# Expert rows added up in pairs on four quarter-size tiles of TensorE's array, in a two-layer hybrid backbone

## The chip, the cores and the metric

The kernel runs on one core of one Trainium2 chip. The metric is the device time of one execution in microseconds (us); of several runs the median is given.

## What is computed

The reference is two layers of a backbone for 128 context tokens and 512 latent tokens of width 1024 (640 tokens, five tiles of 128). Each layer has attention, latent attention and a DeltaNet ahead of one output projection, and then an expert retrieval, which is the part that matters here. All data are float32. Cut to that part:

```python
def peer_ffn(h, w_pq, peer_keys, peer_u, peer_v):
    ...
    experts = jnp.take_along_axis(cand_ix, pos, axis=-1)
    gates = jax.nn.softmax(best, axis=-1)
    def block(args):
        tb, eb, gb = args
        act = jax.nn.gelu(jnp.einsum('nd,nhkd->nhk', tb, peer_u[eb]))
        return jnp.einsum('nhk,nhkd->nd', gb * act, peer_v[eb])
    ...
x = x + gt2 * peer_ffn(h, p['w_pq'], p['peer_keys'], p['peer_u'], p['peer_v'])
```

Every token takes 8 heads x 16 = 128 experts out of 16384. Each expert has a row of 1024 numbers of `peer_u` and a row of 1024 numbers of `peer_v`. The dot product of token and `peer_u` row, through a gelu and times the gate, is the weight with which the `peer_v` row is added to the token's sum.

## The kernel before

A layer is a series of blocks: modulation and projections, DeltaNet, attention, and last `tail`, which holds the output projection, the routing (queries, scores, the choice of experts) and the loop over the experts. `build` calls `tail` for each of the two layers; `finish` follows after the second and computes the final norm.

**The loop over rows.** A "row" of the kernel is one expert for each of the 128 tokens of a token tile: 128 partitions x 2048 numbers (the `peer_u` part in columns 0 to 1023, the `peer_v` part in columns 1024 to 2047), 1 MB. There are ROWS = 640 rows in a layer. They are held in SLOT = 9 buffers, `p.slots[n % 9]` (the trace names them `left` and `right`). A unit is UNIT = 32 rows that are added into the same sum of 128 x 1024; there are UNITS = 20 units in a layer. For row n the engines do this:

- POOL (L1379) waits until row n-9 is released (semaphore `row_free`) and issues the gather of row n as an indirect DMA.
- DVE (L1464) waits for the landing, and computes the 128 dot products into one column of `dot` (128 x 1024 elements read). Behind it comes the product of gelu and gate for the row before, `weigh(n - 1)` (L1440), and then one of the 16 pieces of the choice of experts for a later row group (`top_piece`, L1254 to L1298).
- ACT (L1548) applies the gelu, and then for the row before writes the diagonal (L1541): the identity times the 128 weights, one of DIAGS = 8 buffers of 128 x 128.
- PE (L1646) multiplies the diagonal with the two 512-column halves of the `peer_v` part and adds them into two PSUM banks. The trace shows two MATMUL and two LDWEIGHTS records for each of these matmuls, so four of each for a row. The last one raises `row_free`.

The order on PE is written out by hand: `routing_steps` gives a list of steps and the row ahead of which each is done. A query step (L1602, 8 matmuls of 128 x 512 for the latent tokens) stands ahead of rows 4, 20, 36 and 52 of each block of 128 rows, from the second block on, and at 44, 56, 68 and 80 in the first block. Score steps (L1614) stand ahead of rows 68, 84, 100 and 116, small query steps of 128 columns for the context tokens ahead of some of the first 40 rows. ACT copies a step's result out in `evacuate`, four rows later in its own loop. SP loads the query weights `wq` (L1360, 512 KB each), one buffer of four being free after each step.

**The end of a unit.** Unit u adds into PSUM banks 0 and 1 if u is even and into banks 2 and 3 if u is odd (`sum_banks`). In its loop DVE comes at row 8 of the next unit to `add_unit`: two products of a bank with the gate row `gt2` (L1455, 128 x 512 each) into `y`, and the addition of `y` to the residual `x` (L1457, 128 x 1024). PE waits ahead of the first row of unit u (u of 2 or more) for `y_read` of unit u-2.

Lines that the prediction's steps touch besides: L1509 and L1515 (ACT's copies of 128 x 512 out of PSUM), L1060 and L1062 (score matmuls of the attention; for the differential heads, `kTa` and `qTa`, they use 32 partitions of the contraction, a different group of 32 for each of two following maps), L1089 (a matmul with a 64-column stationary operand), and L234, ACT's 128 x 1024 square at the start of the next layer.

Of the kernel before, what the change touches and what calls it, by code (L numbers as in the profile page):

```python
# [29 lines left out]
ALU = mybir.AluOpType  # L30
# [3 lines left out]
P = 128  # L34
D, L = 1024, 2
# [26 lines left out]
C = 4  # L62
# [1244 lines left out]
def tail(p, lay):  # L1307
# [20 lines left out]

        return c if g == 0 else C + (NT - 1) * c + t - 1

    def sum_banks(u):

        return ps[2 * (u % 2)], ps[2 * (u % 2) + 1]

    def query_bank(m):

# [6 lines left out]
    with nc.Block() as block:  # L1343
        @block.sync
        def _(sp):
            for g in range(2):
                spread(sp, p.rows[:, 0, g, :], d["mid_rows"][0][g:g + 1, :], "load_gt1")
            for g in range(2):
                spread(sp, p.rows[:, 1, g, :], d["mid_rows"][2][g:g + 1, :], "load_sc2")
            spread(sp, p.g2row, d["g_norm2"][bass.ds(lay, 1)], "load_sc2")  # L1350
            for g in range(2):
                spread(sp, p.rows[:, 2, g, :], d["mid_rows"][1][g:g + 1, :], "load_sh2")
            sp.dma_start(p.keysT[:, :], d["keysT"][bass.ds(lay, 1)].rearrange("l p n -> p (l n)")).then_inc(sem("load_keys"), 16)
            for i in range(8 * C):
                if i >= WR:
                    sp.wait_ge(sem("pq_mm"), i - WR + 1)
                if i == 6 * C:
                    sp.wait_ge(sem("y_read"), 2 * C)
                    spread(sp, p.gt2, d["mid_rows"][3][1:2, :], "load_gt2s")
                sp.dma_start(p.wq[:, i % WR, :, :], d["w_pq"][bass.ds(lay, 1), i % (4 * C)].rearrange("l p k n -> p (l k) n")  # L1360
                             ).then_inc(sem(f"load_q{i % WR}"), 16)
                if i == 7:
                    spread(sp, p.gt2, d["mid_rows"][3][0:1, :], "load_gt2")
            for name in p.front_sems:
                sp.sem_clear(sem(name))
# [18 lines left out]
        def _(dve):  # L1384
# [58 lines left out]
            def add_unit(u):  # L1443

                t, _ = unit_of(u)
                dve.wait_ge(sem("row_free"), UNIT * (u + 1))
                if u == 0:
                    dve.wait_ge(sem("load_gt2"), 16)
                if u == C:
                    dve.wait_ge(sem("load_gt2s"), 16)  # L1450
                for c, bank in enumerate(sum_banks(u)):
                    cols = slice(c * 512, c * 512 + 512)
                    if u >= 1:
                        dve.wait_ge(sem("residual"), u)
                    nc.vector.tensor_tensor(p.y[:, cols], bank, p.gt2[:, cols], ALU.mult).then_inc(sem("y_read"), 1)  # L1455
                dve.wait_ge(sem("y_read"), 2 * u + 2)
                nc.vector.tensor_tensor(p.x[:, t, :], p.x[:, t, :], p.y[:, :], ALU.add).then_inc(sem("residual"), 1)  # L1457

            for n in range(ROWS):
# [17 lines left out]
        @block.scalar  # L1477
        def _(act):
            for t in range(NT):
                act.wait_ge(sem("m_turned"), t + 1)  # L1480
                nc.scalar.activation(p.mixedT[t],
                                     ps[t % 2].rearrange("p (k n) -> p k n", k=4), ACT.Copy).then_inc(sem("m_out"), 1)

            def square(t):
                act.wait_ge(sem("res1"), 2 * t + 2)
                nc.scalar.activation(p.junk[:, :], p.x[:, t, :], ACT.Square, accum_out=p.ss1[:, t:t + 1]).then_inc(sem("square2"), 1)
                act.wait_ge(sem("square2"), t + 1)
                nc.scalar.activation(p.rt1[:, t:t + 1], p.ss1[:, t:t + 1], ACT.Sqrt, bias=p.eps[:, 0:1], scale=1.0 / D).then_inc(sem("root2"), 1)

            def turned(t):  # L1490
                act.wait_ge(sem("h2_turned"), t + 1)
                for h in range(2):
                    nc.scalar.activation(p.h2T[:, 4 * h:4 * h + 4, t * P:(t + 1) * P],  # L1493
                                         ps[h].rearrange("p (k n) -> p k n", k=4), ACT.Copy).then_inc(sem("h2T_out"), 1)

            def evacuate(j):

                kind, g, c, i = steps[j]
                if kind == "q":
                    m = block_of(g, c, i)  # L1500
                    act.wait_ge(sem("pq_mm"), m + 1)
                    if g == 0:
                        if c >= 2:
                            act.wait_ge(sem("sc_mm"), c - 1)
                        nc.scalar.activation(p.qp0[:, c % 2, i, :], query_bank(m)[:, 0:P], ACT.Copy).then_inc(sem("q_out"), 1)
                    else:
                        if c >= 1:
                            act.wait_ge(sem("sc_mm"), unit(1, c, 1))
                        nc.scalar.activation(p.qp1[:, i, :], query_bank(m), ACT.Copy).then_inc(sem("q_out"), 1)  # L1509
                else:  # L1510
                    u = unit(g, c, i)
                    act.wait_ge(sem("sc_mm"), u + 1)
                    if u >= SUBS:
                        act.wait_ge(sem("piece"), 1 + MARKS * (2 * (u - SUBS) + 1) + 5)
                    nc.scalar.activation(p.sub[:, u % SUBS, :], score_bank(u), ACT.Copy).then_inc(sem("sub_in"), 1)  # L1515

            early = [j for j in range(len(steps)) if before_row[j] < 0]
            square(0)
            turned(0)
            square(1)  # L1520
            for j in early[0:5]:
                evacuate(j)
            square(2)
            square(3)
            top_gates(p, act, 0)
            square(4)
            turned(1)
            for j in early[5:9]:
                evacuate(j)
            turned(2)  # L1530
            evacuate(early[9])
            turned(3)
            turned(4)
            top_gates(p, act, 1)

            def diag_of(n):

                act.wait_ge(sem("weights"), n + 1)
                if n >= DIAGS:
                    act.wait_ge(sem("row_free"), n - DIAGS + 1)  # L1540
                nc.scalar.activation(p.diag[:, n % DIAGS, :], p.ident, ACT.Copy, scale=p.wgt[:, n % 16:n % 16 + 1]).then_inc(sem("diags"), 1)  # L1541

            j = len(early)
            for n in range(ROWS):
                act.wait_ge(sem("dots"), n + 1)
                if n >= 16:
                    act.wait_ge(sem("weights"), n - 15)
                nc.scalar.activation(p.act2[:, n % 16:n % 16 + 1], p.dot[:, n % 16:n % 16 + 1], ACT.Gelu_apprx_tanh).then_inc(sem("gelus"), 1)  # L1548
                if n >= 1:
                    diag_of(n - 1)  # L1550
                k, s = divmod(n, TOPK)
                if s == 14 and k + AHEAD < ITEMS:
                    top_gates(p, act, k + AHEAD)
                while j < len(steps) and before_row[j] + 4 <= n:
                    evacuate(j)
                    j += 1
            diag_of(ROWS - 1)

        @block.tensor
        def _(pe):  # L1560
# [76 lines left out]
            for n in range(ROWS):  # L1637
                u, s = divmod(n, UNIT)
                while j < len(steps) and before_row[j] <= n:
                    step(j)  # L1640
                    j += 1
                if s == 0 and u >= 2:
                    pe.wait_ge(sem("y_read"), 2 * (u - 1))
                pe.wait_ge(sem("diags"), n + 1)
                for c, bank in enumerate(sum_banks(u)):
                    mm = nc.tensor.matmul(bank, p.diag[:, n % DIAGS, :], p.slots[n % SLOT][:, D + 512 * c:D + 512 * c + 512],  # L1646
                                          start=(s == 0), stop=(s == UNIT - 1))
                mm.then_inc(sem("row_free"), 1)


def finish(p):
# [32 lines left out]
def build(nc, dram):  # L1684

    p = Prog(nc, dram)
    with ExitStack() as ctx:
# [18 lines left out]
        p.io16 = p.cons[:, 4 * P:4 * P + 16]  # L1706
        p.eps = p.cons[:, 4 * P + 16:4 * P + 17]
        p.one = p.cons[:, 4 * P + 17:4 * P + 18]
        for r in range(SLOT):
            p.sem(f"row_in{r}")  # L1710
        start(p)
# [11 lines left out]
def layer(p, lay):  # L1723
# [3 lines left out]
    with ExitStack() as whole:  # L1727
# [90 lines left out]
        with ExitStack() as c1:  # L1818
# [9 lines left out]
            p.qp1 = sb(c1, "qp1", [P, 4, 4 * P])  # L1828
            p.sub = sb(c1, "sub", [P, SUBS, 512])
            p.mixedT = [p.h2T[:, 4 * (t // 4):4 * (t // 4) + 4, P + t % 4 * P:2 * P + t % 4 * P] for t in range(NT)]  # L1830
            p.diag = sb(c1, "diag", [P, DIAGS, P])
            p.y = p.junk
            p.r_top = sb(c1, "r_top", [P, 2, TOPK])
            p.r_ix = sb(c1, "r_ix", [P, 2, TOPK], U32)
            p.r_ixf = sb(c1, "r_ixf", [P, 2, TOPK])
# [14 lines left out]
            p.tail_sems = p.names_of(tail, lay)  # L1850


CONS = 4 * P + 18


def constants():
# [14 lines left out]
    c[:, 4 * P:4 * P + 16] = np.arange(16)  # L1871
    c[:, 4 * P + 16] = EPS
    c[:, 4 * P + 17] = 1.0
    t = np.arange(512)
    n_freq = 8
    freqs = (np.float32(10000.0) ** (-np.arange(n_freq, dtype=np.float32) / n_freq)).astype(np.float32)
# [76 lines left out]
```

## Time and profile before

| what | value |
|---|---|
| median of 3 runs | 5209.98 us (5204.42 to 5218.58) |
| the profiled execution, first to last instruction | 5217.8 us |
| mean granted TensorE clock | 0.963 |
| PE busy | 4403.5 us, 84% |
| DVE busy | 3444.6 us, 66% |
| ACT busy | 1436.0 us, 28% |
| POOL busy | 1498.3 us, 29% |
| bytes moved by DMA | 1481.06 MB, 284 GB/s over the span |
| of these, the gathers of rows (queue q0) | 1342.26 MB |

The profiled execution is one execution of the program. Its span of 5217.8 us lies within the three runs, 7.8 us above their median. The busy time of PE is the time that matmul records cover; they are pipelined, so that a busy PE isn't PE at its peak. A line number is that of the kernel, and for PE the weight loads have a row of their own (PEld). A bracket at the end of a row of the timeline gives the idle time of the engine before it, and what ended that.

### The profile page before, as it was taken

How to read it: one execution, taken by the hardware profiler on the slowest of the kernel's cores; microseconds unless marked ns; L12 is line 12 of the kernel's file. 1: busy time of each engine (PE TensorE's matmuls, PEld its weight loads, DVE VectorE, ACT ScalarE, POOL GpSimd, SP SyncE). 2: the span in 40 equal slices, each digit the busy share in tenths (PEclk: the TensorE clock that was granted, in tenths of full speed). 3: DMA queues.
4: the chain of work that ended last, by engine and by line, in shares of the span. 5: the costliest groups of instructions: out<-in, count | busy, mean ns of one | idle time of the engine just before them, and what ended most of it. 6: DMA issues, size and time to landing. Idle time of an engine off the chain costs nothing. (4 is left out here: it accounts for less than half of the span.)

```text
span 5217.8 us, 51329 instructions
## 1 busy us (share of the span) xinstructions
PE 4403.5 (84%) x14836; PEld 2229.8 (43%) x14836; DVE 3444.6 (66%) x9196; ACT 1436.0 (28%) x4114; POOL 1498.3 (29%) x1410
## 2 busy tenths in 40 slices
PE   7999898888878878887788998988988788897776
PEld 3588665433323323322235886654333233332222
DVE  5555565667676777777565555746677767777775
ACT  2211342222222222222222113522222222222222
POOL 0122100333343434433301220004333334344432
PEclk9988899999999999999999888999999999999999
DMA  7100102899999999999870001019999999999997
GB/s 258 39 3 1 48 1 73 365 418 415 406 416 405 414 420 401 415 419 415 344 258 17 3 1 48 1 73 416 420 414 411 420 404 414 410 405 420 420 414 311
DMA packets 243939, 1481.06 MB, mean 284 GB/s; under 512 B 26384, under 2 KB 32144, under 8 KB 79296
## 3 DMA queue, kind: packets, MB, share of 16 engines
q0 software_dynamic: 184320, 1342.26, 62.5%
q1 hardware_dynamic: 59264, 135.37, 7.2%
q8 instruction: 120, 1.97, 0.2%
q14 instruction: 171, 1.40, 0.1%
q10 hardware_dynamic: 64, 0.07, 0.0%
HBM read 1473.96 MB, written 3.64 MB: 283 GB/s over the span
## 5 line engine op out<-in xcount | busy, mean ns | idle before, releaser
L1646 PE MATMUL psall<-left,diag 128*128 128x512 f32 x2848 | 1373.0, 613 | 323.3 <-ACT diag L1541 322.8
L1646 PE MATMUL psall<-right,diag 128*128 128x512 f32 x2272 | 1105.0, 617 | 265.7 <-ACT diag L1541 265.6
L1379 POOL DMA_INDIRECT left<-in_peer_uv,eidx x712 | 735.8, 1033 | 1797.3 <-PE psall L1646 1058.3
L1464 DVE CUSTOM_DVE_ANT_0 left<-left,mixed 128x1024 f32<-128x1024 f32 x712 | 873.2, 1226 | 543.1 <-DMA left<-in_peer_uv,eidx 543.1
L1646 PEld LDWEIGHTS psall<-left,diag 128*128 128x128 f32 x2848 | 500.1, 190 | 1163.8 <-ACT diag L1541 721.2
L1464 DVE CUSTOM_DVE_ANT_0 right<-right,mixed 128x1024 f32<-128x1024 f32 x568 | 696.8, 1227 | 422.3 <-DMA right<-in_peer_uv,eidx 422.3
L1548 ACT ACTIVATE act<-dot 128x1 f32<-128x1 f32 x1280 | 259.5, 203 | 2411.7 <-DVE dot L1464 2410.7
L1379 POOL DMA_INDIRECT right<-in_peer_uv,eidx x568 | 587.4, 1034 | 884.8 <-PE psall L1646 861.5
L1646 PEld LDWEIGHTS psall<-right,diag 128*128 128x128 f32 x2272 | 401.2, 191 | 945.3 <-ACT diag L1541 597.6
L1541 ACT ACTIVATE diag<-cons,wgt 128x128 f32<-128x128 f32 x1280 | 493.8, 386 | 2.3 <-issue 0.3
L498 POOL TENSOR_TENSOR mlt<-lt,lmask 128x512 f32<-128x512 f32 x120 | 173.0, 1452 | 535.6 <-DVE lt L596 370.8
L1602 PE MATMUL psall<-h2T,wq 128*128 128x128 f32 (+1 forms) x1024 | 286.2, 434 | 4.1 <-ACT h2T L1493 2.5
L1602 PEld LDWEIGHTS psall<-h2T,wq 128*128 128x128 f32 x1024 | 157.4, 191 | 135.4 <-issue 133.6
L1440 DVE TENSOR_TENSOR wgt<-act,gat 128x1 f32<-128x1 f32 x1280 | 196.3, 153 | 0.4 <-ACT act L1548 0.4
L714 PE MATMUL psall<-X,mlt 128*128 128x128 f32 x960 | 143.8, 299 | 44.8 <-DVE XT L626 42.5
L547 ACT ACTIVATE t1s<-psall 128x512 f32<-128x512 f32 x120 | 71.7, 597 | 319.8 <-PE psall L714 319.8
L1151 DVE TENSOR_REDUCE mx<-psall 128x1 f32<-128x640 f32 (+1 forms) x160 | 114.3, 715 | 66.5 <-PE psall L1062 61.1
L625 DVE TENSOR_TENSOR X<-X,psall 128x512 f32<-128x512 f32 x100 | 68.3, 683 | 133.4 <-PE psall L737 133.4
L714 PEld LDWEIGHTS psall<-X,mlt 128*128 128x128 f32 x960 | 127.8, 208 | 56.1 <-issue 55.3
L1129 ACT ACTIVATE prob<-psall,nmax 128x640 f32<-128x640 f32 (+1 forms) x160 | 113.4, 709 | 135.8 <-DVE nmax L1152 135.7
L303 DVE SCALAR_TENSOR_TENSOR qkv<-wlate,sc,qkv 128x512 f32<-128x512 f32 x224 | 149.7, 744 | 0.0
L386 PE MATMUL psall<-wtm,mixed 128*128 128x512 f32 x320 | 142.1, 601 | 8.6 <-PEq L190 5.6
(289 smaller groups left out, 5106.5 us busy)
## 6 DMA issues: line engine op xcount, KB each, us to landing
wlate<-in_w_mod SPq DMA_DIRECT2D x32, 1024.0 KB, 5.3
wq<-in_w_pq SPq DMA_DIRECT2D x64, 512.0 KB, 7.9
left<-in_peer_uv,eidx POOLq DMA_INDIRECT x712, 15.9
right<-in_peer_uv,eidx POOLq DMA_INDIRECT x568, 15.9
w<-in_w_mod SPq DMA_DIRECT2D x4, 2048.0 KB, 10.8
wtm<-in_w_mod SPq DMA_DIRECT2D x4, 2048.0 KB, 18.0
wtm<-in_w_in_tm SPq DMA_DIRECT2D x4, 2048.0 KB, 9.0
right<-in_w_out SPq DMA_DIRECT2D x4, 2048.0 KB, 11.4
```

The costliest lines, as they stand in the source:

```text
L303: late.mark(nc.vector.scalar_tensor_tensor(out=acc, in0=w_late[:, k, :], scalar=p.sc[:, k, g:g + 1], in1=acc, op0=ALU.mult, op1=ALU.add))
L386: mm = p.nc.tensor.matmul(bank, p.hT[:, k, t * P:(t + 1) * P], p.wtm[:, c, k, :], start=(k == 0), stop=(k == KT - 1))
L498: nc.gpsimd.tensor_tensor(p.mlt[:, d, lvl_buf(n), :, :], p.lt[:, d, :, :], bc(p.lmask[:, d, lvl, :], 1, HC), ALU.mult).then_inc(sem(f"mlt{ ...
L714: mm = nc.tensor.matmul(B[0][:, h * P:(h + 1) * P], p.mlt[:, d, lvl_buf(n), h, :], p.X[:, d, h, :], start=True, stop=True)
L1151: own.link(nc.vector.tensor_reduce(p.mx[:, m % 4:m % 4 + 1], p.score2(score_bank(m), nk), AX.X, ALU.max))
L1379: nc.gpsimd.indirect_dma_start(out=p.slots[n % SLOT], out_offset=None, in_=d["peer_uv"], in_offset=bass.IndirectOffsetOnAxis(ap=p.eidx[:, ...
L1440: nc.vector.tensor_tensor(p.wgt[:, n % 16:n % 16 + 1], p.act2[:, n % 16:n % 16 + 1], p.gat[:, t, col:col + 1], ALU.mult).then_inc(sem("wei ...
L1464: nc.vector.tensor_tensor_reduce(out=u_row, in0=u_row, in1=p.mixed[:, t, :], scale=1.0, scalar=0.0, op0=ALU.mult, op1=ALU.add, accum_out=p ...
L1541: nc.scalar.activation(p.diag[:, n % DIAGS, :], p.ident, ACT.Copy, scale=p.wgt[:, n % 16:n % 16 + 1]).then_inc(sem("diags"), 1)
L1548: nc.scalar.activation(p.act2[:, n % 16:n % 16 + 1], p.dot[:, n % 16:n % 16 + 1], ACT.Gelu_apprx_tanh).then_inc(sem("gelus"), 1)
L1602: last = nc.tensor.matmul(query_bank(m)[:, 0:hi - lo], p.wq[:, m % WR, k, :], p.h2T[:, k, lo:hi], start=(k == 0), stop=(k == KT - 1))
L1646: mm = nc.tensor.matmul(bank, p.diag[:, n % DIAGS, :], p.slots[n % SLOT][:, D + 512 * c:D + 512 * c + 512], start=(s == 0), stop=(s == UNI ...
```

## The change

Two following rows n and n+1 (n even) are now added up together. The diagonal of a row is kept as 128 x 64: partitions 0 to 63 hold the first half of the diagonal, partitions 64 to 127 the second half, each as a 64 x 64 diagonal (`fold`, 64 columns more in the constants). Each matmul takes 64 partitions of the row's `peer_v` part and writes 64 partitions of PSUM. For row n the upper half goes to partitions 0 to 63 and the lower half to 64 to 127; for row n+1 the halves are crossed. So the four matmuls for a 512-column half use the four 64 x 64 tiles of the array. Upper halves of tokens are added up in banks 0 and 1, lower halves in banks 2 and 3; in each, even rows and odd rows have partial sums of their own in different partitions. A pair takes 8 matmuls instead of 4, waits for both diagonals, and releases both rows at once.

There is one set of four banks instead of two sets of two. ACT copies the four blocks of 64 x 1024 out to `y` and `ys` (`sums_out`) when its loop comes to row 4 of the next unit; PE waits for these copies ahead of the first row of each unit but the first. DVE at row 8 adds `ys` to `y`, multiplies by `gt2` and adds to `x`, three operations of 128 x 1024 in SBUF.

```diff
-    def sum_banks(u):
-
-        return ps[2 * (u % 2)], ps[2 * (u % 2) + 1]
+    def half_sums(row_half):
+
+        return p.psall[:, 1024 * row_half:1024 * row_half + 1024]
...
-                    sp.wait_ge(sem("y_read"), 2 * C)
+                    sp.wait_ge(sem("y_read"), C)
...
-                dve.wait_ge(sem("row_free"), UNIT * (u + 1))
+                dve.wait_ge(sem("sums_out"), 4 * (u + 1))
...
-                for c, bank in enumerate(sum_banks(u)):
-                    cols = slice(c * 512, c * 512 + 512)
-                    if u >= 1:
-                        dve.wait_ge(sem("residual"), u)
-                    nc.vector.tensor_tensor(p.y[:, cols], bank, p.gt2[:, cols], ALU.mult).then_inc(sem("y_read"), 1)
-                dve.wait_ge(sem("y_read"), 2 * u + 2)
+                nc.vector.tensor_tensor(p.y[:, :], p.y[:, :], p.ys[:, :], ALU.add).then_inc(sem("y_joined"), 1)
+                dve.wait_ge(sem("y_joined"), u + 1)
+                nc.vector.tensor_tensor(p.y[:, :], p.y[:, :], p.gt2, ALU.mult).then_inc(sem("y_read"), 1)
+                dve.wait_ge(sem("y_read"), u + 1)
                 nc.vector.tensor_tensor(p.x[:, t, :], p.x[:, t, :], p.y[:, :], ALU.add).then_inc(sem("residual"), 1)
...
-                nc.scalar.activation(p.diag[:, n % DIAGS, :], p.ident, ACT.Copy, scale=p.wgt[:, n % 16:n % 16 + 1]).then_inc(sem("diags"), 1)
+                nc.scalar.activation(p.diag[:, n % DIAGS, :], p.fold, ACT.Copy, scale=p.wgt[:, n % 16:n % 16 + 1]).then_inc(sem("diags"), 1)
+
+            def sums_out(u):
+
+                act.wait_ge(sem("row_free"), UNIT * (u + 1))
+                if u >= 1:
+                    act.wait_ge(sem("residual"), u)
+                for h in range(2):
+                    for q in range(2):
+                        nc.scalar.activation((p.y, p.ys)[(h + q) % 2][64 * h:64 * h + 64, :], half_sums(h)[64 * q:64 * q + 64, :],
+                                             ACT.Copy).then_inc(sem("sums_out"), 1)
 
             j = len(early)
             for n in range(ROWS):
+                if n >= UNIT and n % UNIT == 4:
+                    sums_out(n // UNIT - 1)
                 act.wait_ge(sem("dots"), n + 1)
...
             diag_of(ROWS - 1)
+            sums_out(UNITS - 1)
...
-                if s == 0 and u >= 2:
-                    pe.wait_ge(sem("y_read"), 2 * (u - 1))
-                pe.wait_ge(sem("diags"), n + 1)
-                for c, bank in enumerate(sum_banks(u)):
-                    mm = nc.tensor.matmul(bank, p.diag[:, n % DIAGS, :], p.slots[n % SLOT][:, D + 512 * c:D + 512 * c + 512],
-                                          start=(s == 0), stop=(s == UNIT - 1))
-                mm.then_inc(sem("row_free"), 1)
+                if s % 2 == 1:
+                    continue
+                if s == 0 and u >= 1:
+                    pe.wait_ge(sem("sums_out"), 4 * u)
+                pe.wait_ge(sem("diags"), n + 2)
+
+                for c in range(2):
+                    for q in range(2):
+                        for h in range(2):
+                            a, b = 64 * h, 64 * ((h + q) % 2)
+                            mm = nc.tensor.matmul(half_sums(h)[b:b + 64, 512 * c:512 * c + 512], p.diag[a:a + 64, (n + q) % DIAGS, :],
+                                                  p.slots[(n + q) % SLOT][a:a + 64, D + 512 * c:D + 512 * c + 512],
+                                                  start=(s == 0), stop=(s == UNIT - 2))
+                mm.then_inc(sem("row_free"), 2)
```

Besides, `diag` shrinks to 128 x 8 x 64, `ys` of 128 x 1024 is new, and the table of constants has 64 columns more.

## Rows read from the trace of the kernel before

**Rows 1.** The page, part 2: granted clock and DMA share in 40 slices, tenths
```profile
PEclk9988899999999999999999888999999999999999
DMA  7100102899999999999870001019999999999997
```

**Rows 2.** Windows: busy us (instructions) by engine, granted clock, DMA share, GB/s
```profile
1400.00:1600.00 200.00, 158.95 (x359) 60.68 (x359) 142.14 (x424) 55.55 (x181) 78.15 (x78) 1.00 1.01 416
1600.00:1800.00 200.00, 171.16 (x379) 67.34 (x377) 140.71 (x419) 54.13 (x176) 79.77 (x77) 1.00 1.00 406
2575.00:2600.00 25.00, 19.94 (x41) 7.15 (x42) 11.90 (x28) 4.88 (x20) 2.79 (x3) 1.00 0.50 196
2600.00:2625.00 25.00, 5.64 (x28) 4.38 (x26) 6.42 (x12) 10.28 (x17) 0.00 (x0) 0.66 0.45 144
```

**Rows 3.** Timeline, one row of steady state: start us, us, engine, line
```profile
1704.45 1.23 DVE L1464 CUSTOM_DVE_ANT_0 right<-right,mixed 128x1024 f32<-128x1024 f32 x1 [0.62 <-DMA right<-in_peer_uv,eidx]
1705.83 0.39 ACT L1541 ACTIVATE diag<-cons,wgt 128x128 f32<-128x128 f32 x1
1706.27 1.98 PE L1646 MATMUL psall<-right,diag 128*128 128x512 f32 x4 [0.41 <-ACT diag L1541]
1706.94 1.22 DVE L1464 CUSTOM_DVE_ANT_0 right<-right,mixed 128x1024 f32<-128x1024 f32 x1 [0.66 <-DMA right<-in_peer_uv,eidx]
1708.53 0.94 POOL L1379 DMA_INDIRECT right<-in_peer_uv,eidx  x1 [1.46 <-PE psall L1646]
```

**Rows 4.** Issues of the gathers on POOL (L1379): waits, and time to landing
```profile
  PE psall L1646: 1919.8, 1172
DMA to landing us min/median/max: 6.1/15.9/23.3
```

**Rows 5.** Timeline around one query step
```profile
1628.44 7.03 PE L1602 MATMUL psall<-h2T,wq 128*128 128x512 f32 x16
1637.46 0.94 POOL L1379 DMA_INDIRECT left<-in_peer_uv,eidx  x1 [7.65 <-PE psall L1646]
```

**Rows 6.** Timeline of PE in the attention, maps on 96 and on 32 partitions
```profile
627.17 2.04 PE L1060 MATMUL psall<-kTb,qTb 96*128 96x512 f32 x2 [0.98 <-PEq L863]
629.57 2.08 PE L1060 MATMUL psall<-kTa,qTa 32*128 32x512 f32 x4
631.44 0.64 PE L1062 MATMUL psall<-kTa,qTa 32*128 32x128 f32 x4
632.01 1.22 PE L1060 MATMUL psall<-kTb,qTb 96*128 96x512 f32 x1
```

**Rows 7.** Timeline at the end of the first layer's rows
```profile
2580.67 0.94 POOL L1379 DMA_INDIRECT left<-in_peer_uv,eidx  x1 [0.30 <-issue]
2596.09 1.23 DVE L1464 CUSTOM_DVE_ANT_0 left<-left,mixed 128x1024 f32<-128x1024 f32 x1 [1.18 <-DMA left<-in_peer_uv,eidx]
2597.47 0.72 ACT L1541 ACTIVATE diag<-cons,wgt 128x128 f32<-128x128 f32 x2
2597.91 3.70 PE L1646 MATMUL psall<-left,diag 128*128 128x512 f32 x8 [0.50 <-ACT diag L1541]
2601.65 1.29 DVE L1455 TENSOR_TENSOR junk<-psall,gt 128x512 f32<-128x512 f32 x2 [3.89 <-PE psall L1646]
2602.97 1.22 DVE L1457 TENSOR_TENSOR x<-x,junk 128x1024 f32<-128x1024 f32 x1
2612.42 1.06 ACT L234 ACTIVATE junk<-x 128x1024 f32<-128x1024 f32 x1
```

**Rows 8.** Groups by line, 1400 to 2200 us: busy us, mean ns
```profile
L1509 ACT ACTIVATE qp<-psall 128x512 f32<-128x512 f32 x9 | 5.2, 575 | 0.0
```

**Rows 9.** The page, parts 1 and 3: records by engine; instruction queue, packets, MB, share
```profile
PE 4403.5 (84%) x14836; PEld 2229.8 (43%) x14836; DVE 3444.6 (66%) x9196; ACT 1436.0 (28%) x4114; POOL 1498.3 (29%) x1410
...
q8 instruction: 120, 1.97, 0.2%
```

**Rows 10.** Groups of weight loads by line, whole execution
```profile
L1089 PEld LDWEIGHTS psall<-probT,vb 128*64 128x64 f32 x672 | 72.5, 139 | 26.0 <-ACT probT L1114 13.2 <-ACT probT L1112 5.9 <-issue 0.4
```

More of the change, by code:

```diff
@@ L1708, in build @@
         p.one = p.cons[:, 4 * P + 17:4 * P + 18]
+        p.fold = p.cons[:, 4 * P + 18:4 * P + 82]
         for r in range(SLOT):
@@ L1830, in layer @@
             p.mixedT = [p.h2T[:, 4 * (t // 4):4 * (t // 4) + 4, P + t % 4 * P:2 * P + t % 4 * P] for t in range(NT)]
-            p.diag = sb(c1, "diag", [P, DIAGS, P])
+            p.diag = sb(c1, "diag", [P, DIAGS, 64])
             p.y = p.junk
+            p.ys = sb(c1, "ys", [P, D])
             p.r_top = sb(c1, "r_top", [P, 2, TOPK])
@@ L1850, in layer @@
             p.tail_sems = p.names_of(tail, lay)
-CONS = 4 * P + 18
+CONS = 4 * P + 18 + 64
 def constants():
@@ L1873, in constants @@
     c[:, 4 * P + 17] = 1.0
+    c[:, 4 * P + 18:] = (i[:, None] % 64 == np.arange(64)[None, :])
     t = np.arange(512)
```

## The prediction

> **What bounds the kernel now.** I read the slices of the page first. In the last dozen slices of each layer, where the rows of experts are added up, the DMA digit stands at 9 and TensorE's clock at 9 or full [rows 1]. The windows sharpen this: in 200 us pieces of that stage the DMA share is 1.00 to 1.01 at 406 to 416 GB/s, while PE, DVE and ACT are busy 171, 142 and 56 of 200 us at most in the pieces shown [rows 2] (two of six such pieces stand there). The timeline of one row gives the rhythm: a dot product starts every 2.49 us, each time after DVE had waited 0.6 us for a landing. 1.05 MB at 416 GB/s are 2.5 us. So a row costs what its transfer costs. Counting from the start of the dot product of row n+1, the diagonal of row n is done after 1.77 us, its four matmul records run from 1.82 to 3.80 us, and POOL issues into the freed buffer at 4.08 us [rows 3]. POOL's waits are all for PE [rows 4], which looks like a bound by PE. It isn't: a gather lands 15.9 us (median) after its issue, and 6.1 us are enough when little is queued [rows 4]. So some 10 us, four rows, of queue lie between the release of a buffer and the need for it. Even a query step of 7.03 us on PE, which delays an issue by 7.65 us [rows 5], fits into that.
>
> A quicker PE therefore buys nothing in the steady state. What the change can do is to eat the queue, and to lengthen the end of each layer, which nothing hides.
>
> **The pair on PE.** It removes 8 matmul records per pair and adds 16 on tiles of a quarter of the array. Eight more records raise 1.98 us by the difference of the rows of 3.70 and 1.98 us for each four, so a record of 512 columns takes 0.43 us at the 2.4 GHz level [rows 3, 7]. If all four tiles run at once, a pair takes 16/4 x 0.43 + 0.2 (start and end) = 1.9 us; at the 1.2 GHz level 3.6 us. If only two run at once, 3.6 and 7.1 us; if none does, 7.1 us at the high level. The attention shows what tiles of different rows do: a map on 96 partitions takes from 627.17 to 629.57, 2.40 us, and two maps on 32 partitions each, in different row groups, together take from 629.57 to 632.01, 2.44 us. The program has the two 128-column records of the first map ahead of the second map's 512-column ones, yet all four long records stand ahead of the first short one [rows 6]. So two row tiles overlap wholly, and one tile doesn't hold up the other. Tiles that differ in columns alone are not in the trace. I take four at once, because the row tiles behave as independent arrays.
>
> The Trainium skill says otherwise of the order (TensorE: Matmul & The Clock Gate, Part 3): matmuls keep strictly to program order in start and in end. By that a tile's first record would wait for its neighbour's second and a pair would take 3.6 us; the rows above speak against it. For column tiles only the skill has a statement (TensorEngine Tiling (Array Packing), Key Properties): different tiles run in parallel, which would give the 1.9 us.
>
> Weight loads: 16 of 64 columns at 139 ns [rows 10] are 2.2 us if they ran one by one, 0.6 us if by tiles; the pair takes 1.9 to 2.2 us, and 1.9 is taken. In steady state all of this is hidden: the pair starts when its second diagonal is ready, and the even row is released 2.5 us later than now, the odd one at the same time, out of 10 us of queue.
>
> **TensorE's clock.** Now PE pauses 0.4 us between rows and is granted 1.00 [rows 2, 3]. Where it had no work, from 2601.6 us on, the mean of the stretch was 0.66 [rows 2], so part of it at the 1.2 GHz level. After the change it pauses 5.0 - 1.9 = 3.1 us between pairs and some 9 us at each unit's start. I expect the low level there, and cost the first pair of a unit at 3.6 us.
>
> **The new wait at each unit's start.** Let 0 be the start of row 0's dot product, 2.5 us a row. ACT is through with iteration 3 at 7.5 + 1.77 = 9.3 us, and then makes four copies of 64 x 1024 out of PSUM. Bounds: 128 x 1024 from SBUF took 1.06 us [rows 7], two copies of 128 x 512 would take 2 x 0.575 = 1.15 us [rows 8]; following each other they overlap a little, so I take 1.0, four 4.0 us. PE waits for them until 13.3 us. The pair (0,1) would have started at 6.8. It now ends at 16.9; row 9 is issued at 17.2 and with 6.1 us lands at 23.3, where it is due at 22.5: 0.8 us late, or 0.9 us early if the clock is high. Queued behind that wait on PE are the pair (2,3) and, in 7 of 19 unit starts per layer, the query step ahead of row 4: pair to 18.8 or 20.5, step to 25.8 or 27.5, pair (4,5) to 27.7 or 29.4, row 13 issued 0.3 later and landed at 34.1 to 35.8. It is due at 32.5, plus 1.25 us for the 512 KB of query weights, 33.75: 0.35 to 2.05 late, middle 1.2. In all per layer 12 x 0.8 + 7 x 1.2 = 18 us, 36 for both. That is if 6.1 us were what an empty queue takes; it is only the least that was seen, and includes what that row waited. Lower end 0, upper end 36 + 38 x 4 x 0.15 (copies of 1.15 us) = 59. I take 10, nearer the lower end, as one pair at the high clock level already clears most starts.
>
> ACT's own queue: gelu(4) and diagonal 3 wait behind the copies until 13.3 us, 1.9 us late; the diagonal is of a row that PE can't take before then. DVE's weigh(4) needs gelu(4) at 13.65: not late. ACT is busy 28%, so the 4 us are made up by row 5. POOL and SP wait for nothing new; SP's wait for `y_read` has the same meaning.
>
> **DVE at row 8.** Three operations of 1.22 us, 3.7 us, for 1.29 + 1.22 = 2.5 us [rows 7]. The 1.2 us more per unit fall into DVE's waits for landings, 0.6 us a row, two rows; and the rows delayed keep their buffers 1.2 us longer, out of the queue. Cost 0; without cover 38 x 1.2 = 46 us.
>
> **The end of a layer, covered by nothing.** Now: last diagonals at 2598.19, matmuls to 2601.61, DVE to 2604.19 [rows 7]. After: pair 2598.25 to 2600.15 or 2601.85, middle 2601.0; four copies to 2605.1; DVE 3 x 1.22 + gaps 3.8, to 2608.9. That is 4.7 us later (3.8 to 6.2), 9.4 for two layers.
>
> **Instructions.** PE has 2 x 14836 = 29672 records; queue q8 brings 1.97 MB of instructions in 120 packets [rows 9], if it is PE's 66 bytes a record. 640 pairs x 16 more records are 0.68 MB, 41 packets. 0.2% of 16 engines' span are 167 us, 1.4 us a packet: 57 us if all fell on the DMA engine that ends last, 57/16 = 4 if spread. I take 4, since gathers too are spread over all 16. The 32 KB more of constants: 0.1 us.
>
> **Sum.** 9.4 + 10 + 4 = 23 us. The profiled execution would go from 5217.8 (its span is 7.8 above the median) to 5241; from the median of 5210.0, 5233 us. About 0.3%, 16 us, is what a measurement of this kernel can tell from no change.
>
> **Rivals.** *Only the ends cost* (the queue never runs dry, fetches are lost in noise): 5210 + 9 = 5219. For: the lateness was worked out with the longest bounds. Chance 0.21. *Tiles overlap by twos only* (by column tiles waiting, or by the order rule): pair 3.6, at the low clock 7.1. Row 9 is issued at 20.7 and 4.3 us late; starts with a query step lose about 9 us. 24 x 4.3 + 14 x 9 = 229, with 13 for the rest 5450. Against: rows 6. Chance 0.12. *No overlap*, the change doesn't do what it says: 7.1 us a pair against 5.0 of transfer, 640 x 2.1 = 1340, 6550 us; chance 0.03. *Faster*: the windows with query steps move 406 instead of 416 GB/s [rows 2]; if DMA runs dry behind each of these steps on the path that ends last, a PE that clears its backlog at 1.9 instead of 3.7 us a pair gets it back: 2.4% of 200 us for four steps, 1.2 us each, 32 steps, 39 us; 5210 - 39 + 13 = 5184. It decides if issue to landing falls to 6.1 us behind those steps. For: the rates. Against: the median of 15.9 us, and that at the layer's end the last landing came 15.4 us after the last issue though DMA was half idle already [rows 2, 7]: some engine is far behind the mean, and that one never ran dry. Chance 0.09.
>
> **The numbers.** Forecast 0.55, of which 0.43 is over 5226. Its own range is 5212 (no wait costs) to 5290 (59 us at unit starts and part of the 57). Slower: 0.43 + 0.12 + 0.03 = 0.58; same: 0.12 + 0.21 = 0.33; faster 0.09. The range from 5180 takes in the faster case and leaves out 0.15 above.
>
> **What would show it.** Right: pair's 16 records in 1.9 to 3.6 us, dot products still every 2.49 us, DMA share 1.00; clock below 1.00 in this stage; PE idle for ACT's copies about 9 us at 38 places; the last dot product of a layer to DVE's last addition 12.8 instead of 8.1 us. Wrong: pairs over 3.6 us at the high level; DVE's waits for landings of many us after unit starts; a last dot product of the first layer ahead of 2596 us.

## The result, and the profile of the changed kernel

The changed kernel takes 5271.23 us (median of 4 runs, 5268.99 to 5274.95); the kernel before, run beside it, 5212.14 us (4 runs, 5204.42 to 5218.58). The ratio is 1.0115, with a 95% interval of 1.0101 to 1.0129: 59 us slower, where 23 were forecast. The profiled execution took 5271.15 us with a span of 5269.3.

The page, parts 1, 2 and 3 (engines, slices, the queue of instructions):

```profile
PE 3692.9 (70%) x19956; PEld 1762.0 (33%) x19956; DVE 3487.0 (66%) x9196; ACT 1530.0 (29%) x4274; POOL 1666.5 (32%) x1410
...
PEclk9988899877778878777799888997777777787776
DMA  7100101999999999999870001029999999999997
...
q8 instruction: 160, 2.62, 0.2%
```

TensorE is busy 711 us less than in [rows 9], and the kernel is slower. Its clock, full in the row stages of [rows 1], is now granted at 7 or 8 tenths there, so part of the time at the 1.2 GHz level. The instruction queue has 40 more packets. The DMA digits look as before; only the rates of the windows tell the difference.

Windows of the changed kernel, columns as in [rows 2]:

```profile
1400.00:1600.00 200.00, 116.59 (x660) 32.86 (x664) 143.68 (x422) 59.04 (x187) 93.16 (x79) 0.77 1.00 409
1600.00:1800.00 200.00, 125.95 (x656) 36.58 (x648) 140.86 (x411) 59.62 (x185) 89.61 (x74) 0.81 1.00 408
...
1400.00:2400.00 1000.00, 594.60 (x3308) 168.44 (x3312) 721.31 (x2100) 297.81 (x933) 451.55 (x385) 0.77 0.99 406
```

The same 1000 us of the kernel before:

```profile
1400.00:2400.00 1000.00, 817.76 (x1799) 313.06 (x1799) 719.20 (x2132) 275.48 (x901) 402.15 (x390) 0.99 1.00 413
```

POOL, which in this stretch does nothing but issue gathers, has issued 385 rows instead of 390 in that time. So most of the loss is in the row stages. From the first issue of a layer's rows to the last landing it took 1668.0 and 1665.0 us before, and 1685.5 and 1684.8 now: 37.3 us more.

The timeline of the changed kernel shows a pair in the steady stretch, one unit's start, and the end of the first layer (lines between are left out; the trace calls the buffer `y` by the name `junk`):

```profile
1904.71 1.95 PE L1663 MATMUL psall<-right,diag 64*64 64x512 f32 x16 [1.35 <-ACT diag L1539]
...
2121.54 1.22 DVE L1462 CUSTOM_DVE_ANT_0 left<-left,mixed 128x1024 f32<-128x1024 f32 x1
...
2130.40 1.00 ACT L1548 ACTIVATE junk<-psall 64x1024 f32<-64x1024 f32 x1
...
2131.43 2.06 ACT L1548 ACTIVATE ys<-psall 64x1024 f32<-64x1024 f32 x2
2133.51 1.02 ACT L1548 ACTIVATE junk<-psall 64x1024 f32<-64x1024 f32 x1
...
2134.58 4.40 PE L1663 MATMUL psall<-left,diag 64*64 64x512 f32 x18 [9.34 <-ACT junk L1548]
...
2138.57 0.94 POOL L1379 DMA_INDIRECT left<-in_peer_uv,eidx  x1 [10.24 <-PE psall L1663]
...
2139.81 1.43 POOL L1379 DMA_INDIRECT left<-in_peer_uv,eidx  x1 [0.30 <-issue]
...
2612.97 1.23 DVE L1462 CUSTOM_DVE_ANT_0 left<-left,mixed 128x1024 f32<-128x1024 f32 x1 [1.18 <-DMA left<-in_peer_uv,eidx]
2618.13 1.02 ACT L1548 ACTIVATE junk<-psall 64x1024 f32<-64x1024 f32 x1 [3.11 <-PE psall L1663]
2619.17 2.06 ACT L1548 ACTIVATE ys<-psall 64x1024 f32<-64x1024 f32 x2
2621.25 1.02 ACT L1548 ACTIVATE junk<-psall 64x1024 f32<-64x1024 f32 x1
2622.30 1.23 DVE L1451 TENSOR_TENSOR junk<-junk,ys 128x1024 f32<-128x1024 f32 x1 [7.67 <-ACT junk L1548]
2623.56 1.23 DVE L1453 TENSOR_TENSOR junk<-junk,gt 128x1024 f32<-128x1024 f32 x1
2624.82 1.23 DVE L1455 TENSOR_TENSOR x<-x,junk 128x1024 f32<-128x1024 f32 x1
```

The pair's 16 records take 1.95 us: the four tiles run at once. At the unit's start, counted from its first dot product at 2121.54, ACT copies from 8.9 to 13.0 us, and TensorE, which had waited 9.34 us, starts at 13.0. Its first pair runs at the low level, so row 9 is issued only at 17.0 and row 10 at 18.3. At the end of the layer it is 13.1 us from the last dot product (2612.97) to the end of DVE's last addition (2626.05). In [rows 7] it was 8.1. At the end of the second layer it is 12.0 us, against 8.1 again in the kernel before.

The gathers' issues (L1379) in 1400 to 2400 us, changed kernel:

```profile
  PE psall L1663: 467.0, 154
DMA to landing us min/median/max: 5.5/12.6/16.3
```

The kernel before, same view and stretch:

```profile
DMA to landing us min/median/max: 9.8/15.9/18.1
```

So the queue is about 3 us shorter throughout, which costs nothing by itself (in e1 and e5 below it is 12.9 and 12.6, without the loss), and at some places it is down to 5.5 us. The landing times of all rows in the trace say at which. Over all 38 unit starts, row 9 takes 5.6 us (median) from issue to landing and lands 22.8 us after the unit's first dot product, 0.4 late. The next row then lands 3.45 us behind it instead of 2.49. Row 10 is due at 24.9 (10 x 2.493) and lands 1.3 us late (median). Not all of that is the change's: in the kernel before row 9 lands 0.7 and row 10 0.75 us behind the same due times. The rows' intervals separate the two. Added up over the 38 starts, the intervals that end with the landings of rows 9 and 10 are 52 us over 2.493 us each in the changed kernel (16 and 36) and 7 us in the kernel before (4 and 3). The DMA engines show the gap itself: averaged over the 38 starts, their busy share is 0.71, 0.35 and 0.83 in the microseconds from 17 to 20 after the first dot product, where the kernel before has 1.01, 1.01 and 1.01. Row 8 is then still on its way; it lands 2.7 us (median) after row 9's issue.

### The profile page after: what moved, and what is told of

It is laid out like the page before. It is cut to its first block and busy times, and to the rows that moved or that the text cites. A ratio compares the mean times of both kernels' runs of the same rounds, so it can differ in the third digit from the quotient of the medians.

```text
span 5269.3 us, 61737 instructions
## 1 busy us (share of the span) xinstructions
PE 3692.9 (70%) x19956; PEld 1762.0 (33%) x19956; DVE 3487.0 (66%) x9196; ACT 1530.0 (29%) x4274; POOL 1666.5 (32%) x1410
## 5 line engine op out<-in xcount | busy, mean ns | idle before, releaser
L1663 PE MATMUL psall<-left,diag 64*64 64x512 f32 x5696 | 1161.7, 813 | 782.7 <-ACT diag L1539 585.5
L1379 POOL DMA_INDIRECT left<-in_peer_uv,eidx x712 | 830.1, 1166 | 1787.9 <-PE psall L1663 929.9
L1663 PE MATMUL psall<-right,diag 64*64 64x512 f32 x4544 | 951.4, 797 | 557.8 <-ACT diag L1539 413.6
L1379 POOL DMA_INDIRECT right<-in_peer_uv,eidx x568 | 661.2, 1164 | 773.0 <-PE psall L1663 662.4
L1663 PEld LDWEIGHTS psall<-left,diag 64*64 64x64 f32 x5696 | 278.9, 169 | 1466.3 <-ACT diag L1539 874.3
L1663 PEld LDWEIGHTS psall<-right,diag 64*64 64x64 f32 x4544 | 228.0, 166 | 1094.4 <-ACT diag L1539 654.5
L1539 ACT ACTIVATE diag<-cons,wgt 128x64 f32<-128x64 f32 x1280 | 425.7, 333 | 1.8 <-issue 0.3
## 6 DMA issues: line engine op xcount, KB each, us to landing
left<-in_peer_uv,eidx POOLq DMA_INDIRECT x712, 12.6
w<-in_w_mod SPq DMA_DIRECT2D x4, 2048.0 KB, 10.5
```

The source lines that it names most:

```text
L1379: nc.gpsimd.indirect_dma_start(out=p.slots[n % SLOT], out_offset=None, in_=d["peer_uv"], in_offset=bass.IndirectOffsetOnAxis(ap=p.eidx[:, ...
L1539: nc.scalar.activation(p.diag[:, n % DIAGS, :], p.fold, ACT.Copy, scale=p.wgt[:, n % 16:n % 16 + 1]).then_inc(sem("diags"), 1)
L1663: mm = nc.tensor.matmul(half_sums(h)[b:b + 64, 512 * c:512 * c + 512], p.diag[a:a + 64, (n + q) % DIAGS, :], p.slots[(n + q) % SLOT][a:a + ...
```

## The experiments

Ten kernels were run. Theory A throughout: TensorE's wait for the copies at a unit's start holds back the release of buffers until the gathers' queue runs dry, that is, until the DMA engines have hardly anything left to move before the next gather comes. The rivals are named with each. Medians of before are those of the runs beside each.

**The copies two rows earlier (e1) and one row earlier (e5).** Edit in the changed kernel, for e1 (e5 has 3 in place of 2):

```diff
-                if n >= UNIT and n % UNIT == 4:
+                if n >= UNIT and n % UNIT == 2:
```

> The changed kernel with ACT's four copies of a unit's sums made at row 2 of the next unit instead of row 4. Theory A (PE waits at each unit's start for these copies, so that the first rows' buffers come free too late and the gathers run dry): the copies start 2.4 to 4.8 us earlier, row 9 is issued near 13.3 instead of 17.0 us after the unit's first dot product, its issue-to-landing time goes from 5.6 to 9 us and more, and the some 37 us lost in the two row stages come back: 5230 to 5240 us. Theory B (the 16 more records per pair, their instruction fetches or the switching of tile modes cost it): the copies' place doesn't matter, 5271 within 5 us.

> The changed kernel with the copies of a unit's sums at its fourth row instead of its fifth; nothing else differs. TensorE's wait at a unit's start then ends near 10.6 us after the unit's first dot instead of 13.1, row 9 is issued near 14.4 instead of 17.0, 8 us before it is due, and after a query step row 13 is issued near 25.2 to 26.8. Theory A (the price of the wait begins only where a load is issued later than its 5.5 us before it is due, and then has a restart of the empty queue in it): no row is late, so the same as with the copies at the third row, 5222 to 5228 us, and the median from issue to landing at a unit's start falls from 9.6 to some 7 us without cost. Theory B (each us of wait costs in proportion, from the third row's 5222 to the fifth row's 5271): 5240 to 5250.

e1 took 5222.24 us (10 runs; ratio 1.0022, 1.0009 to 1.0035), e5 5222.69 us (10 runs; 1.0021, 1.0005 to 1.0036). The timeline of e5 at the same unit's start, and under it its row of the windows:

```profile
2114.11 4.53 PE L1663 MATMUL psall<-left,diag 64*64 64x512 f32 x18 [5.48 <-ACT junk L1548]
...
2118.11 0.94 POOL L1379 DMA_INDIRECT left<-in_peer_uv,eidx  x1 [6.51 <-PE psall L1663]
```

```profile
1400.00:2400.00 1000.00, 607.11 (x3364) 170.68 (x3364) 730.78 (x2139) 303.28 (x949) 450.26 (x389) 0.78 1.01 412
```

The bracket counts from the end of TensorE's work before it, which isn't the same in the two kernels; counted from the unit's first dot product, the copies end at 10.7 us (median of the 38 starts) instead of 13.2. With a wait that is only 2.5 us shorter, and the low clock as it was (0.78), the whole loss of the row stages is gone: 389 rows in the window, and 1666.2 and 1663.9 us for the two stages. Over the 38 starts, rows 9 and 10 are 9 us over 2.493 each, instead of 52, and the DMA share stays at 0.84 or more throughout. In e1 the copies end at 9.2 us, but TensorE then waits for a diagonal until 9.8, so that row 9 is issued at 13.6 instead of 14.7 us. This further 1 us gains nothing. So the wait costs 5271.2 - 5222.5 = 49 us, and it costs nothing up to a limit. The proportional rival (5240 to 5250 for e5) falls. e1 came out under the 5230 to 5240 expected of it, because I had taken more than the ends of the layers for lasting.

**The copies two rows later (e2).** Edit: `n % UNIT == 6` in the same line.

> The copies at row 6 instead of row 4. Theory A: PE starts each unit 5 us later, with no queue left, so each of 38 starts costs nearly 5 us more: 5271 + 190 = 5460 us. Theory B: 5271 to 5280 us.

5460.02 us (1.0475, 1.0456 to 1.0494). Its row of the windows:

```profile
1400.00:2400.00 1000.00, 566.06 (x3180) 162.41 (x3175) 682.21 (x1974) 281.24 (x880) 428.85 (x365) 0.77 0.93 383
```

Two rows are 5.0 us more of waiting, and 5460.0 - 5271.2 = 189 us are 5.0 us at each of 38 starts. Past the limit every microsecond counts in full. If it does so from the limit on, the 1.3 us (49/38) lost at the fifth row put the limit 1.3 us before the 13.2 us at which the copies end there, at 11.9; e5, at 10.7, lies below it.

**The wait without the tiles (e3).** The kernel before, its 128 x 128 matmuls kept, with one pair of banks for all units and ACT's copies after iteration 3, made twice so that they take as long as the four; DVE then multiplies and adds in SBUF (two operations):

```diff
-        return ps[2 * (u % 2)], ps[2 * (u % 2) + 1]
+        return ps[0], ps[1]
...
+            def sums_out(u):
...
+                for again in range(2):
...
+                    for h in range(2):
+                        nc.scalar.activation(p.y[64 * h:64 * h + 64, :], p.psall[64 * h:64 * h + 64, 0:1024],
+                                             ACT.Copy).then_inc(sem("sums_out"), 1)
...
-                if s == 0 and u >= 2:
-                    pe.wait_ge(sem("y_read"), 2 * (u - 1))
+                if s == 0 and u >= 1:
+                    pe.wait_ge(sem("sums_out"), 4 * u)
```

> The kernel before with its own 128 x 128 matmuls, but one set of two banks, copied out by ACT at row 4 (four copies of 64 x 1024, each half twice, so that they take as long as in the changed kernel), and PE waiting for them at each unit's start. DVE multiplies and adds in SBUF. Theory A: the wait alone costs, and without the quicker pairs more than in the changed kernel: rows 0 and 1 at the low clock level end near 20 us, a query step at row 4 makes row 13 some 4 us late; 5300 to 5320 us, 10 of it at the ends of the layers. Theory B: only the ends cost, 5222 us.

5311.62 us (1.0191, 1.0172 to 1.021), as expected. The wait alone, on the old matmuls, costs 100 us over the kernel before; with the tiles the whole change costs 59. The tiles are not the cause. They soften it, since a backlog of rows is cleared at 1.9 us for two at the high clock level instead of 3.7.

**TensorE kept busy in its wait (e4).** The result of the added matmuls goes into a bank that nobody reads before it is written anew:

```diff
+                    pe.wait_ge(sem("q_out"), sum(step[0] == "q" for step in steps[:j]))
+                    for _ in range(6):
+                        nc.tensor.matmul(ps[4], p.ident, p.h2T[:, 0, P:P + 512], start=True, stop=True)
```

> The changed kernel, with six matmuls of 128 x 512 into a query bank, whose result nobody reads, ahead of PE's wait at each unit's start (5 to 7 us of work in a wait of 9.3 us). Theory A with the clock (the first pair takes 3.5 us since PE idled, and these 1.6 us are what makes row 9 late): the first pair takes 1.95 us, row 9 is issued 1.6 us earlier, 1 us comes back at each of 38 starts: 5230 to 5240 us. If the clock doesn't matter: 5271 us. If the dummy matmuls overrun the wait: slower.

5243.99 us (1.0065, 1.0044 to 1.0086). The timeline of e4 at the same unit's start:

```profile
2111.33 5.58 PE L1658 MATMUL psall<-h2T,cons 128*128 128x512 f32 x12
...
2118.36 1.02 ACT L1548 ACTIVATE junk<-psall 64x1024 f32<-64x1024 f32 x1
...
2119.43 2.36 PE L1666 MATMUL psall<-left,diag 64*64 64x512 f32 x18 [2.52 <-ACT junk L1548]
...
2121.68 1.48 POOL L1379 DMA_INDIRECT left<-in_peer_uv,eidx  x1 [7.25 <-PE psall L1666]
```

The copies end at the same time as in the changed kernel (13.2 us after the first dot product, median of both). Row 9 is issued 2.30 us later (2119.38 to 2121.68), where the changed kernel needed 4.04 us (2134.53 to 2138.57). In the changed kernel it is 3.7 to 4.05 us at all 38 starts: TensorE comes out of the wait at the low level every time. In e4 it is 2.3 to 3.0 us at 22 starts and 3.2 to 4.0 us at 16; by the granted clock the pair began at the high level at 29 starts, and at 8 of these it fell to the low one within 1.5 us. The landings go with it: rows 9 and 10 together are 0.3 us over 2 x 2.493 at the 22 starts and 1.0 us at the 16, where the changed kernel has 1.4 and e5 0.2. 22 of 38 starts mended are 28 of 49 us; 27 were measured. So what ran the queue dry was the wait and the slow first pair behind it together; either cured alone is enough.

**The loads' lead, in the kernel before (e6, e9) and with pairs (e7, e10).** The lead of a load is the time from its issue until it is due. Edit: fewer slots for the rows, in e6 and e9 of the kernel before (7 and 6), in e7 and e10 of e1 (7 and 8); the buffers' room in memory stays:

```diff
-SLOT = 9
+SLOT = 7
...
-            p.left = sb(c1, "left", [P, SLOT - 4, 2 * D])
+            p.left = sb(c1, "left", [P, 5, 2 * D])
```

> The kernel before with 7 slots for the loaded rows instead of 9, the row tiles of TensorE, the two banks and the ends of layers as before. Theory A (what the queue needs is that a load is issued over 5.5 us before it is due, and nothing else of the depth matters): from issue to landing a row takes some 10.9 instead of 15.9 us in the steady stretch, and about 7 behind a query step, still above 5.5, so 5212 to 5225 us. Theory B (depth itself is what the changed kernel lost at unit starts: any issue nearer to its due time costs): over 5250 us.

> The changed kernel with the copies at the third row (5222 us with 9 slots, where a row at a unit's start took 9.6 us from issue to landing) and 7 slots instead of 9. TensorE waits no longer than there. Theory A (the lead of a load over its due time decides): the lead at a unit's start falls by two rows, 5.0 us, to 4.6, under the 5.5 that a load needs, so 1 to 2 us are lost at each of the 38 starts: 5260 to 5300 us, although the wait is the short one. Theory B (the length of TensorE's wait decides, by its clock or its own backlog): 5220 to 5230.

> The kernel before with 6 slots. Left open by the run of the changed kernel with 7 slots (5504 us: 8 to 10 us from issue to landing in its steady stretch, 6 at unit starts): is it the short lead of the loads alone that costs, or that pairs free and fill the slots two at a time? By the runs with 9 and 7 slots (15.9 and 10.9 us) a row here takes 8.4 us from issue to landing, one every 2.5 us. Theory A (only a lead under some 5.5 us costs; two at a time is what made 8 to 10 too little): nothing in the steady stretch, 1 to 2 us at the steps of the next unit's queries, 5250 to 5300 us. Theory B (a lead under some 9 us costs in itself, however the loads are spaced): over 5400 us.

> The changed kernel with the copies at the third row and 8 slots: between 9 slots (5222 us) and 7 (5504 us). Each row has 2.5 us less from issue to due time than with 9: some 10.5 to 12 us in the steady stretch and 7 at unit starts. Theory A (a gentle threshold: a unit start of 5.6 us cost 1.2 us, one of 7.8 nothing): 5222 to 5240 us. Theory B (pairs need two rows in flight at every moment, and the steady stretch already stands close to the edge): 5260 to 5350 us.

Measured, with the issue-to-landing times and rates of 1400 to 2400 us (each ratio is to the runs of the kernel before beside it, so the medians of different rows compare only roughly):

| kernel | buffers freed | slots | median us (ratio) | issue to landing, min/median | GB/s |
|---|---|---|---|---|---|
| before | singly | 9 | 5212 | 9.8/15.9 | 413 |
| e6 | singly | 7 | 5228.62 (1.0036) | 5.4/10.9 | 410 |
| e9 | singly | 6 | 5338.86 (1.0240) | 5.5/8.4 | 396 |
| e5 | in pairs | 9 | 5222.69 (1.0021) | 6.6/12.6 | 412 |
| e10 | in pairs | 8 | 5242.74 (1.0055) | 5.6/10.5 | 409 |
| e7 | in pairs | 7 | 5504.22 (1.0577) | 5.5/8.9 | 378 |

Two slots less cost the kernel before 19 us of 5209.5, and e10 stands 25 over its 5218.0, 12 to 14 more than e5 and e1 over theirs (13.2 and 10.6): the threshold of theory A, a little outside the numbers given (up to 5225 and 5240). e7 is a miss by 200 us. The landings of its rows put about 88 of its some 280 lost us at rows 7 and 8 of a unit (2.3 us each time); the rest is spread over the unit, with 34 us at its rows 15 and 37 at its rows 27. e9 tells why the short lead alone isn't the cause. Its rows land 8.4 us after their issue too, yet in the steady stretch it loses nearly nothing. Its loss is at the rows held up by the query steps, which stand ahead of rows 4 and 20 of a unit: rows 10 and 26 of the units, together 108 of the 265 us that its row stages are over 2.493 us a row, where the kernel before has 133 in all and 6 in these two rows. The difference shows in POOL's rows of the timelines. e7 issues in twos, the next two 3.4 to 5.2 us behind:

```profile
2002.83 1.47 POOL L1379 DMA_INDIRECT right<-in_peer_uv,eidx  x1 [1.98 <-PE psall L1663]
...
2004.61 0.93 POOL L1379 DMA_INDIRECT right<-in_peer_uv,eidx  x1 [0.30 <-issue]
...
2009.76 1.87 POOL L1379 DMA_INDIRECT right<-in_peer_uv,eidx  x1 [4.21 <-PE psall L1663]
...
2011.93 0.94 POOL L1379 DMA_INDIRECT right<-in_peer_uv,eidx  x1 [0.30 <-issue]
...
2015.35 1.26 POOL L1379 DMA_INDIRECT left<-in_peer_uv,eidx  x1 [2.48 <-PE psall L1663]
```

e9, here behind one query step, issues one by one as rows are added:

```profile
2006.31 0.94 POOL L1379 DMA_INDIRECT right<-in_peer_uv,eidx  x1 [7.64 <-PE psall L1646]
...
2011.46 0.93 POOL L1379 DMA_INDIRECT right<-in_peer_uv,eidx  x1 [0.66 <-PE psall L1646]
...
2013.17 0.94 POOL L1379 DMA_INDIRECT right<-in_peer_uv,eidx  x1 [0.79 <-PE psall L1646]
```

I read this as the queue falling low between two pairs of e7, since for up to 5 us nothing is issued, about what a gather needs. That reading is argued; no run spaces the issues of pairs out. A rival stands beside it: the granted clock from 1400 to 2400 us is 0.75 in e7 and 0.99 in e9, and at the low level a pair releases its buffers 1.7 us later. No run keeps the two apart. e9's 5339 us lies between its two theories (5250 to 5300, over 5400): the place is A's, the price is higher.

**A shorter end of the layer (e8).** e1, where at a layer's last unit DVE multiplies the two blocks that need no crossing straight out of the banks while ACT copies the crossed ones:

```diff
+                if u == UNITS - 1:
...
+                    for h in range(2):
+                        nc.vector.tensor_tensor(p.y[64 * h:64 * h + 64, :], half_sums(h)[64 * h:64 * h + 64, :],
+                                                p.gt2[64 * h:64 * h + 64, :], ALU.mult).then_inc(sem("y_joined"), 1)
```

> The changed kernel with the copies at the third row, and at the last unit of a layer alone VectorE multiplies the two blocks that need no crossing straight out of the banks while ScalarE copies the two crossed ones. Behind a layer's last matmul stand then two copies (2.1 us) and VectorE's two full operations instead of four copies and three: 11.2 instead of 13.1 us from the last dot. Theory A (the 10.6 us left over 5212 with the copies at the third row are the ends of the two layers): 2 to 4 us less, 5218 to 5220. Theory B (they lie in the row stages): no change, 5222.

5226.04 us (10 runs; 1.0022, 1.0008 to 1.0036). The timeline of e8 at the end of the first layer:

```profile
2594.84 1.23 DVE L1475 CUSTOM_DVE_ANT_0 left<-left,mixed 128x1024 f32<-128x1024 f32 x1 [1.18 <-DMA left<-in_peer_uv,eidx]
...
2598.95 2.48 DVE L1449 TENSOR_TENSOR junk<-psall,gt 64x1024 f32<-64x1024 f32 x2 [2.45 <-PE psall L1678]
...
2603.92 1.23 DVE L1457 TENSOR_TENSOR x<-x,ys 128x1024 f32<-128x1024 f32 x1
```

The end takes 10.3 us (2594.84 to 2605.15) in both layers, where e1, from which e8 differs, takes 12.5 and 12.0: 3.9 us less for the two. The median didn't move (5222.24 and 5226.04). A gain of 4 us is below what separates two medians here: the stretch ahead of the first gather alone took 928 us in the profiled execution of the kernel before and 917 in that of e1. So this run decides nothing about what is left. No version beat the kernel before.

## Why the prediction was wrong in size

**Right: what bounds it, and that a quicker PE buys nothing.** 711 us less of TensorE's time gave no time back; in e1 and e5 the row stages are within 2 us of those of before.

**Right: the tiles.** 1.9 us per pair at the high level was forecast and 1.95 measured; 3.6 at the low one was forecast and up to 3.7 measured (3.69 at 2150.24 us). The rivals with tiles by twos or none (5450, 6550 us) fall by that row. By the Trainium skill (TensorE: Matmul & The Clock Gate, Part 3) matmuls keep program order in start and end, which would have made it 3.6 at the high level; the 1.95 us of this trace speak against that for tiles.

**Right: the ends.** 12.8 us forecast, 13.1 and 12.0 measured in the two layers, against 8.1: 8.9 us for both, 9.4 forecast. With the wait's cost removed, e1 and e5 stand 10.6 and 13.2 us over their before, of which their ends are 8.3 and 8.6. That agrees within what medians here can tell; it was not shown separately, as e8 could not resolve it.

**Wrong: the term of the unit starts.** The walk to the issue was right. Copies end at 13.3 (13.2 measured), row 9 is issued at 17.2 (17.2, median of 38), and it lands at 23.3 (22.8). From that walk I had worked out 36 us, and then took 10, "nearer the lower end, as one pair at the high clock level already clears most starts". The measured term is 49. Two things failed:
- The clock. Not one of the 38 starts had its first pair at the high level. I had written in the part on the clock that I expected the low level there, and then argued the term down with the high one. e4 shows what that argument would have been worth had it held: 27 us came back with the pair quick at 22 of the 38 starts.
- What a dry queue costs. I counted the lateness of row 9 alone. Measured, row 9 is 0.4 us late (0.7 in the kernel before), and row 10 is 1.3 late (0.75 before), because the gather behind the dry spell lands 3.45 us after its forerunner instead of 2.49. Of the 44 us that rows 9 and 10 lose against the kernel before, 32 are at row 10. At the starts with a query step row 13 adds about 1.4 us each, 19 us in the two layers, where the kernel before has 3; other rows, where the kernel before loses a little, make part of it all good again, which is how the stages come to 37. I had doubted that an empty queue takes as much as 6.1 us. With row 8 still on its way it took 5.6 (median), but in e2, where row 8 had landed 2.3 us before row 9's issue, 6.0. So the doubt was no ground for taking less than 36 either.

**Not separable: the instructions.** 40 packets came, 41 were forecast; the 4 us put on them lie below the resolution. In the profiled executions 37.3 us of the row stages and 8.9 of the ends make 46 of 51.5; the other 5 were not traced to anything.

**The other rivals.** "Only the ends cost" (5219) is near what e1 and e5 are (5222 and 5223); it would have been right with the copies one row earlier. "Faster" wanted the queue to run dry behind the query steps of the kernel before. It doesn't: with the tiles and no dry starts, the row stages of e5 are 1 to 2 us shorter, not 20 each. That pricing of DVE's 1.2 us more per unit at nothing was right, as e1 has the same three operations.

## What to carry to other kernels

When work is bound by a queue of loads, price a new wait by the lead of the load issued behind it: due time minus issue, less what a gather needs. In these runs it cost nothing up to that edge and about every microsecond past it (0, 49 and 238 us for copies at the fourth, fifth and seventh row). Walk it with the clock level that the engine has after the idle time that the wait itself makes, and when the walk gives a number, keep it: with 36 in place of 10 the forecast would have been 49 us more, where 59 were measured. With buffers freed in twos this kernel needed more of them than with buffers freed singly, at about the same median from issue to landing (e7 and e9); whether the twos alone do it was not shown.

## What the runs showed of the hardware

- Four tiles of 64 x 64 of the array, different in rows and columns, run at once: 16 fp32 records of 512 columns in 1.95 us, 0.43 us a record as for the full array, and the tiles' first records start within 20 ns of each other.
- A gather of 1 MB issued when only the one before is still on its way (landing 2.7 us later) lands after 5.6 us (median of 38, 5.4 to 6.4); issued 2.3 us after the one before had landed (e2), after 6.0 us (5.6 to 7.9). The one issued 1.2 us behind it in the changed kernel lands 3.45 us later still (median), where a full queue lands one every 2.49 us. Why the second is slow was not looked into.
- After some 9 us without a matmul, TensorE ran its first pair at the 1.2 GHz level at all 38 starts, and in e1, after 4.8 to 6.1 us, at all 38 too. With 5.6 us of other matmuls in the wait (e4) it began the pair at 2.4 GHz at 29 of them and held that level at 21.
- ACT copies 64 x 1024 fp32 from PSUM in 1.018 us (median; 999 to 1022 ns over 160 copies); half the partitions save nothing over the 1.06 us of 128 x 1024 from SBUF [rows 7]. Nor do they on DVE, where two products of 64 x 1024 took 2.48 us one behind the other in e8.
